# A gate unit between the value units, two levels of masks drawn ahead, and decay rows in two parts, in the gated delta stage of a two-block decoder

## The reference

```python
def c_mixer(h, w_in, conv_w, a_log, dt_bias, head_gain, w_out):
    qkv, gate, b, a = _split(h @ w_in, C_SIZES)
    qkv = jax.nn.silu(short_conv(qkv, conv_w))
    ...
    o = gated_deltanet(q, k, v, beta, log_alpha)
    o = rmsnorm(o, head_gain) * jax.nn.silu(gate.reshape(B, T, GDN_HEADS, GDN_DV).astype(jnp.float32))
    return o.reshape(B, T, GDN_VW) @ w_out

def gated_deltanet(q, k, v, beta, log_alpha):
    g = jnp.cumsum(_to_chunks(log_alpha.astype(f32), L), axis=-1)
    decay = jnp.where(incl, jnp.exp(g[..., :, None] - g[..., None, :]), 0.0)
    kk = jnp.einsum('nbhtd,nbhsd->nbhts', kc, kc)
    lower = jnp.where(strict, bc[..., :, None] * kk * decay, 0.0)
    rhs = jnp.concatenate([vc * bc[..., None], kc * (bc * jnp.exp(g))[..., None]], axis=-1)
    sol = lax.linalg.triangular_solve(lower + eye, rhs, ...)
    attn = jnp.einsum('nbhtd,nbhsd->nbhts', qc, kc) * decay
    ...  # then a scan over the chunks
```

## Time and profile before

| | |
|---|---|
| median of 3 runs | 1335.72 us (1333.64 to 1336.63) |
| profiled execution, its own time | 1339.24 us |
| its span, first to last instruction | 1337.2 us |
| PE busy | 1279.0 us (96%) |
| weight loads on PE | 1161.5 us (87%) |
| DVE, ACT, POOL busy | 790.7, 707.8, 128.2 us (59%, 53%, 10%) |
| mean granted TensorE clock | 0.984 |
| read from HBM | 203.05 MB, 153 GB/s over the span |

### The profile page before, as it was taken

One profiled execution on the slowest core, in us unless ns is written; L12 is line 12 of the kernel. 1 busy time (PEld: TensorE's weight loads), 2 busy tenths in 40 slices (PEclk: granted clock), 3 DMA queues, 4 the chain that ended last, 5 costly groups with the idle time before them and its releaser, 6 DMA issues.

```text
span 1337.2 us, 22102 instructions
## 1 busy us (share of the span) xinstructions
PE 1279.0 (96%) x9192; PEld 1161.5 (87%) x9192; DVE 790.7 (59%) x1159; ACT 707.8 (53%) x1115; POOL 128.2 (10%) x146
## 2 busy tenths in 40 slices
PE   6999999999999979999999999998999999999997
PEld 6988899998889868888998888988997888999886
DVE  5776678885456565655554447784555645555444
ACT  5766666664476434645555336562355544655443
POOL 5000001110000000000111000106500000111000
PEclk9999999999999999999999999997999999999999
DMA  9433455555544523533655554541112543455550
GB/s 331 154 113 117 142 190 186 177 176 203 188 126 174 189 95 126 189 127 98 198 179 189 193 182 147 173 140 48 66 33 83 186 158 126 158 181 178 194 200 37
DMA packets 141430, 205.53 MB, mean 154 GB/s; under 512 B 3730, under 2 KB 118802, under 8 KB 141330
## 3 DMA queue, kind: packets, MB, share of 16 engines
q1 hardware_dynamic: 141330, 204.11, 46.0%
HBM read 203.05 MB, written 1.05 MB: 153 GB/s over the span
## 4 chain that ended last, share of the span: by engine, by line
PE 85%; DVE 7%; ACT 4%; issue 2%; DMA 1%; SPq 0%; POOL 0%; ACTq 0%; DVEq 0%
PE ps L301 41%; PE ps L363 26%; PE ps L381 5%; PE ps L2055 2%; DVE weights_lo L280 2%; PE ps L1703 1%; PE ps L2120 1%; ACT weights_hi L277 1%; PE ps L1725 1%; PE ps L2006 1%; PE ps L2010 1%; PE ps L485 1%; DVE split_arena L516 1%; ACT normed L902 1%; DMA weights<-in_w_in 1%
## 5 line engine op out<-in xcount | busy, mean ns | idle before, releaser
L280 DVE TENSOR_TENSOR weights_lo<-weights,weights_hi 128x1024 fp32r<-128x1024 f32 x379 | 471.3, 1255 | 248.9 <-ACT weights_hi L277 247.0
L301 PE MATMUL ps<-split_arena,weights_hi 128*128 128x256 f32 x3056 | 565.8, 287 | 7.9 <-DVE split_arena L516 7.0
L277 ACT ACTIVATE weights_hi<-weights 128x1024 fp32r<-128x1024 f32 x379 | 396.7, 1057 | 267.1 <-PE ps L363 183.0
L301 PEld LDWEIGHTS ps<-split_arena,weights_hi 128*128 128x128 f32 x3056 | 483.2, 194 | 16.2 <-issue 11.9
L301 PE MATMUL ps<-split_arena,weights_lo 128*128 128x256 f32 x1528 | 435.5, 285 | 0.0
L301 PEld LDWEIGHTS ps<-split_arena,weights_lo 128*128 128x128 f32 x1528 | 296.5, 194 | 0.0
L363 PE MATMUL ps<-weights_hi,split_arena 128*128 128x512 f32 x992 | 272.6, 392 | 5.1 <-DVE arena L1649 3.0
L363 PEld LDWEIGHTS ps<-weights_hi,split_arena 128*128 128x128 f32 x992 | 184.5, 188 | 44.4 <-issue 6.1
L363 PE MATMUL ps<-weights_lo,split_arena 128*128 128x512 f32 x496 | 153.6, 390 | 0.0
L363 PEld LDWEIGHTS ps<-weights_lo,split_arena 128*128 128x128 f32 x496 | 93.1, 188 | 19.6
L1883 POOL TENSOR_TENSOR normed<-normed 128x512 f32<-128x512 f32 x32 | 34.1, 1065 | 502.9 <-ACTq L1875 502.9
(11 more groups left out here) (358 smaller groups left out, 1332.8 us busy)
## 6 DMA issues: line engine op xcount, KB each, us to landing
weights<-in_mlp_w SPq DMA_DIRECT2D x64, 1024.0 KB, 5.4
weights<-in_w_up SPq DMA_DIRECT2D x22, 1024.0 KB, 5.1
weights<-in_c_w_in SPq DMA_DIRECT2D x16, 1024.0 KB, 5.5
weights<-in_w_in SPq DMA_DIRECT2D x14, 1024.0 KB, 6.2
weights<-in_ab_w_in SPq DMA_DIRECT2D x12, 1024.0 KB, 5.3
weights<-in_w_down SPq DMA_DIRECT2D x11, 1024.0 KB, 5.0
weights<-in_xa_wv SPq DMA_DIRECT2D x8, 1024.0 KB, 4.9
weights<-in_xa_wq SPq DMA_DIRECT2D x8, 1024.0 KB, 5.3
```

The source lines that it names most:

```text
L277: act.activation(h, r, ACT.Copy).then_inc(s_hi, 1)
L280: dve.tensor_tensor(l, r, h.bitcast(F32), ALU.subtract).then_inc(s_lo, 1)
L301: mm = pe.matmul(o, w[:, k, :], x[:, k, :], start=(k == 0 and i == 0), stop=(k == DC - 1 and i == 2))
```

## The change

The stage computes the same with its work placed otherwise:

- **Order of units.** The first gate unit comes between the value units, as `c_gate0`, and its columns go to bank 4; ACT copies them out before `products(0)`. The gate columns are turned between the two parts of the last value unit, and DVE copies them out ahead of its last `conv`. What was `gate_part(0)` and `(1)` is gone; `gate_part(2)` to `(7)` keep their numbers. The key tile of one part (`keys(1, 1)`) comes ahead of that of two.
- **Decay rows.** `CRK` and `CRQ` are split by DVE into high and low fp32r parts (`RBK`, `RBQ`); `products(n)` takes two heads at all 256 tokens instead of four heads at 128, as four fp32r matmuls of 128x256, whose stationary operand is a column of an 8x8 identity, repeated (`SELR`).
- **Masks.** POOL makes levels 0 and 1 of `hg` 0, then both of `hg` 1, then the two subtractions (`XT`). `products(4)` moves ahead of level 1.
- **Splits.** In levels 1 to 4 the parts that are split are one further along the list than before (`GP0 + 7 + lvl`), so ACT's high part there waits for the `gate_part` of its own level; the split before the scan is gone.
- **End.** Head squares and sums have four buffers, three head sums come first, then the key tile of one part, the fourth head sum and the key tile of two parts; DVE and ACT copy them out in that order.

```diff
-            cols("c_qkv", "c_w_in", [*range(1024, 2048, 256), *range(0, 1024, 256), *range(2048, 3072, 256)])
-            cols("c_gate", "c_w_in", range(3072, 4096, 256))
-            keys(1, 0, 1)
+            cols("c_qkv", "c_w_in", [*range(1024, 2048, 256), *range(0, 1024, 256), 2048, 2304])
+            cols("c_gate0", "c_w_in", [3072])
+            cols("c_v", "c_w_in", [2560, 2816])
+            cols("c_gate", "c_w_in", range(3328, 4096, 256))
+            keys(1, 1, 0)
...
-        CRK, CRQ = PIN_t[0:8, 0, :], PIN_t[0:8, 1, :]
+        CRK, CRQ = GS[1], GS[2]
+        RBK = view(44 * 256, (2, T), 8, of=split_arena)
+        RBQ = view(46 * 256, (2, T), 8, of=split_arena)
+        SELR = sb("head_rows", [8, 8], F32R)
...
-        GP0 = first_part[first_unit["c_gate"]]
+        GP0 = first_part[first_unit["c_gate"]] - 2
...
+        def unit_at(u):
+            return ("c_qkv", u) if u < 10 else ("c_v", u - 10)
+
+        def heads_at(n):
+            return n % 4 // 2, n % 2 * 2
...
-            for u in range(NCU):
-                cols_unit("c_qkv", u, HT, G + u % 4, free)
+            def gate_columns():
+                pe.wait_ge(named("c_row"), 2)
+                for t in range(TT):
+                    pe.transpose(PS[:, A + 3, 72 * t:72 * t + 72], GAB[:, t * P:(t + 1) * P], ident[0:72, 0:72])
+                pe.matmul(PS[:, A + 3, 144:152], ones[0:8, :], DG[:, :], start=True,
+                          stop=True).then_inc(named("c_cols"), 1)
+
+            for u in range(NCU - 1):
+                if u == 10:
+                    cols_unit("c_gate0", 0, HT, A)
+                stage, i = unit_at(u)
+                cols_unit(stage, i, HT, G + u % 4, lambda _i: free(u))
                 for i in SQUARES_AFTER.get(u, ()):
                     sum_squares(i)
...
+            free(11)
+            cols_part(first_unit["c_v"] + 1, 0, HT, G + 3)
+            gate_columns()
+            cols_part(first_unit["c_v"] + 1, 1, HT, G + 3)
 
             def products(n):
...
-                hg, c = n // 2 % 2, n % 2
-                r, q0 = (CRK, 8) if n < 4 else (CRQ, 0)
+                hg, j0 = heads_at(n)
+                r, q0 = (RBK, 8) if n < 4 else (RBQ, 0)
                 if n == 0:
                     pe.wait_ge(named("c_silu"), 8)
+                    pe.wait_ge(named("c_ge"), 1)
...
-                for j in range(4):
-                    mm = pe.matmul(PS[:, MB[n], j * P:(j + 1) * P], sel[:, 4 * hg + j, :], r[:, tok(c)], start=True,
-                                   stop=True)
+                for i in range(2):
+                    h = 4 * hg + j0 + i
+                    one = SELR[:, h:h + 1].to_broadcast([8, P])
+                    for x in range(2):
+                        mm = pe.matmul(PS[:, MB[n], i * T:(i + 1) * T], one, r[:, x, :], start=(x == 0),
+                                       stop=(x == 1))
                 mm.then_inc(named("c_p"), 1)
...
             products(0)
             products(1)
             products(2)
-            gate_part(0)
+            gate_part(2)
             products(3)
-            gate_part(1)
-            gate_part(2)
-
-            pe.wait_ge(named("c_lt"), 2)
+            gate_part(3)
+
+            pe.wait_ge(named("c_lt"), 3)
             pe.wait_ge(named("c_prep"), 2)
             blocks(6, lambda r, hg, m: LT[r, 0, hg, m, :], lambda r, hg, m: ident[r, r], "c_ym")
-            gate_part(3)
+            products(4)
 
             for lvl in range(1, LEVELS):
                 pe.wait_ge(named("c_x"), 2 * lvl)
                 pe.wait_ge(named("c_lt"), 2 * lvl + 2)
-                if lvl == 1:
-                    pe.wait_ge(named("c_prep"), 3)
                 blocks(2, lambda r, hg, m: LT[r, lvl % 2, hg, m, :], lambda r, hg, m: XI[r, hg, m, :], "c_ym")
                 if lvl < 5:
-                    products(3 + lvl)
+                    if lvl > 1:
+                        products(3 + lvl)
                     gate_part(3 + lvl)
                     value_turn(lvl - 1)
                     pe.wait_ge(named("c_prep"), 4 + lvl)
...
-                    if lvl % 2 == 0:
-                        pe.wait_ge(named("c_tq"), lvl // 2)
+                    pe.wait_ge(named("c_tq"), lvl)
...
 
             head_sums(0)
             head_sums(1)
-            key_pe(1, 0, 4)
             head_sums(2)
+            key_pe(1, 1, 5)
             head_sums(3)
-            key_pe(1, 1, 5)
+            key_pe(1, 0, 4, lambda: pe.wait_ge(named("c_rs"), 3))
...
+            act.wait_ge(s_const, 2)
+            act_then(act.activation(SELR[:, :], ident[0:8, 0:8], ACT.Copy))
             for u in range(NCU):
-                cols_done(act, "c_qkv", u)
+                if u == 10:
+                    cols_done(act, "c_gate0", 0)
+                    act.activation(SGT[:, 0:2, :], PS[:, A, :].rearrange("p (c n) -> p c n", c=2),
+                                   ACT.Copy).then_inc(named("c_ge"), 1)
+                cols_done(act, *unit_at(u))
...
-            split(act, GP0 + 3)
+            split(act, GP0 + 5)
             decays(3)
             act.wait_ge(named("c_row"), 3)
...
-            split(act, GP0 + 4)
-            gate_evac(0)
-            split(act, GP0 + 5)
             split(act, GP0 + 6)
             gate_evac(1)
+            decays(4)
+            query_decay(0)
+            split(act, GP0 + 7)
             for lvl in range(1, LEVELS):
                 y_high(lvl)
                 if lvl < 5:
-                    decays(3 + lvl)
-                    if lvl % 2 == 0:
-                        query_decay(lvl // 2 - 1)
-                    split(act, GP0 + 6 + lvl)
+                    if lvl > 1:
+                        decays(3 + lvl)
+                        query_decay(lvl - 1)
+                    split(act, GP0 + 7 + lvl)
...
+            for b in range(4):
+                head_squares(b)
+            for b in range(3):
+                head_roots(b)
             out_high(0)
-            key_evac(1, 0, act, 4)
-            head_roots(2)
             out_high(1)
             head_roots(3)
-            split(act, GP0 + 13)
+            split(act, GP0 + 12)
             out_high(2)
             out_high(3)
+            split(act, GP0 + 13)
+            key_evac(1, 0, act, 4)
...
-            for lvl in range(LEVELS):
+            def masked(lvl, hg):
+                for b in range(2):
+                    r = slice(64 * b, 64 * b + 64)
+                    ins = pool.tensor_tensor(LT[r, lvl % 2, hg, :, :], ATC[r, hg, :, r],
+                                             LM[r, lvl, r].unsqueeze(1).to_broadcast([64, 8, 64]), ALU.mult)
+                ins.then_inc(named("c_lt"), 1)
+
+            pool.wait_ge(named("c_silu"), NCU)
+            for hg in range(2):
+                pool.wait_ge(named("c_prep"), 2 * hg + 2)
+                masked(0, hg)
+                masked(1, hg)
+            for hg in range(2):
+                pool.wait_ge(named("c_lt"), 4)
+                pool_then(pool.tensor_tensor(XT[:, hg, :, :], idb, LT[:, 0, hg, :, :], ALU.subtract))
+                pool.sem_inc(named("c_xt0"), 1)
+            for lvl in range(2, LEVELS):
...
+                dve_then(dve.tensor_copy(RBK[:, 0, :], CRK))
+                dve.tensor_tensor(RBK[:, 1, :], CRK, RBK[:, 0, :].bitcast(F32), ALU.subtract)
...
+                dve_then(dve.tensor_copy(RBQ[:, 0, :], CRQ))
+                dve_then(dve.tensor_tensor(RBQ[:, 1, :], CRQ, RBQ[:, 0, :].bitcast(F32), ALU.subtract))
...
-            for u in range(NCU):
+            for u in range(NCU - 1):
                 conv(u)
                 if u == ROWS_AFTER:
                     gate_rows()
-
             dve.wait_ge(named("c_cols"), 1)
             dve_then(dve.tensor_copy(GCB[:, :, :], PS[:, A + 3, 0:144].rearrange("p (t n) -> p t n", t=2)))
             dve_then(dve.tensor_tensor(GX[:, 0, :], PS[:, A + 3, 144:152], GCB[:, 0, 0:8], ALU.subtract))
             dve.sem_inc(named("c_row"), 1)
+            conv(NCU - 1)
...
             exponents(1)
             decayed(0)
             exponents(2)
-            split(dve, GP0 + 3)
             decayed(1)
             exponents(3)
             decayed(2)
             decayed(3)
-            split(dve, GP0 + 4)
             split(dve, GP0 + 5)
+            split(dve, GP0 + 6)
...
-            split(dve, GP0 + 6)
+            exponents(4)
+            decayed(4)
+            split(dve, GP0 + 7)
...
-                if lvl < 5:
+                if 1 < lvl < 5:
                     exponents(3 + lvl)
                     decayed(3 + lvl)
-                    split(dve, GP0 + 6 + lvl)
+                if lvl < 5:
+                    split(dve, GP0 + 7 + lvl)
...
-            split(dve, GP0 + 12)
             out_low(0)
             gate_out(2)
             out_low(1)
-            split(dve, GP0 + 13)
+            key_evac(1, 1, dve, 5)
+            split(dve, GP0 + 12)
             gate_out(3)
             out_low(2)
-            key_evac(1, 1, dve, 5)
```

(1 more changed line is left out.)

106 lines of the change are left out of this document (39 added, 67 removed).

## The result

| | before | changed |
|---|---|---|
| median, runs on one chip | 1336.57 us (7 runs, 1333.64 to 1341.07) | 1329.45 us (7 runs, 1326.29 to 1330.54) |
| ratio of times, 95% interval | | 0.994 (0.9924 to 0.9956) |
| profiled execution, its own time | 1339.24 us | 1329.45 us |
| its span | 1337.2 us | 1327.6 us |
| mean granted clock | 0.984 | 0.985 |

The change makes the kernel faster, by 0.6% or some 8 us (5.9 to 10.2 by the interval; the two medians differ by 7.1). The forecast was 1324.3 with 1319.5 to 1331.0: the time is inside, 5.2 us above the forecast.

A forecast was written before the change was run, and what follows sets the result against it. PE, busy for 96% of the span, was the bound, with 16.4 us of idle time and half clock between 883.17 and 941.79. Gains of 7.8 + 0.9 + 2.7 = 11.4 us off the median 1335.72 gave 1324.3, range 1319.5 to 1331.

The forecast's parts named there:

- A: From the start of the eleventh unit to level 1's blocks(4): 7.8 us gained, bounds 3.4 to 10.2.
- A, columns: PE idles 0.8 us ahead of the first value unit's second part, 0.4 ahead of products(2), where 2.9 stood.
- A, spreading rows: In products, four fp32r matmuls take 0.5 us instead of 1.06; 0.121 us each, upper bound 0.28.
- A, masks: Level 0's blocks(6) waits for six half masks: 6.3 us idle, start 920.8; two splits meeting masks add 1.8.
- A, clock: Clock falls in PE's idle before blocks(6), returns 8 to 9 us after PE resumes; level 1's blocks(4) at 934.0.
- B: Levels 2 to 4: products 0.56 us shorter each, less 0.8 us lost; gain 0.9 us, bounds -0.5 and 1.7.
- The feared delay of X: Levels 1 and 2: DVE's low-part split meeting a mask delays X by 0.7 us, 0.3 hidden; 0.8 us lost.
- C: End of the stage: of c_out's 2.8 us wait for a key tile copy 0.1 stays; gain 2.7, bounds 1.2 and 2.8.
- the first two rivals: Clock low through level 1: 1328.7, chance 0.15; all masks slow, X late in all levels: 1329.1, chance 0.08.

The follow-up runs named there:

- fp32 rows: Changed kernel with decay rows spread by fp32 matmuls of 256 columns, without DVE's four extra gate-row instructions; 1326.94 us, ratio to before 0.9927.
- changed kernel's second trace: Profile of the changed kernel timed again with no edit; median 1328.73 us, ratio to before 0.9939, stage 145.2 us.
- end alone: Kernel before with only four buffers of head squares and sums and the new end order of key tiles, copies and units; 1333.04 us, ratio 0.9977.
- the second execution: Profile of the kernel before, run again with no edit; median 1338.37 us, ratio 1.0013, stage 154.0 us.
- the old masks: Changed kernel with POOL's mask order of before (level 0 of both groups, subtractions, then level 1); 1329.23 us, ratio to before 0.9932.

## Why the prediction was right, and where its sizes were off

The direction, the mechanism and each place that it named hold. The sizes are off in places, and some of the agreement is luck.

- **A, columns.** 0.8 us of idle ahead of the value part: 0.71. 0.4 ahead of `products(2)`: 0.21, a little less because the rows took longer.
- **A, spreading rows.** I priced them at 0.121 us each by L301. They take 0.67 / 4 = 0.17 us: type and width were not all that sets them. It lies between my bounds, but the upper one, 0.28, was an fp32 matmul of 128 columns; of 256 columns it takes 0.53 (two in 1.06 us, in "fp32 rows"). It cost 0.2 us per `products`, hidden in the first four.
- **A, masks.** `blocks(6)` at 920.8 forecast, 921.09 measured; its wait 6.3 forecast, 5.8 measured. The charge of 1.8 us for two splits is 1.7 by experiment, and masks beside other work of DVE were not slow: in the changed kernel's second trace four that ran beside the copy of Y, exponents and `decayed` of level 2 took 5.31 us, 1.33 each. By the rule in the Trainium skill, "GPSIMD Engine Reference", section 1, splits with two SBUF inputs contend and exponents out of PSUM do not; these rows agree.
- **A, clock.** Back 8 to 9 us after PE resumed, I said; it was 929.8 - 921.1 = 8.7. I had taken that from one low stretch of the trace of before, and other waits brought 3.4 or 13.6 us, so part of this agreement is luck. `blocks(4)` at 934.0 forecast, 934.23 measured. My bounds doubled the work for half clock; the rows show less, 3.68 for 2.08 us of `blocks` and 0.64 for 0.36 of three matmuls of a weight part. A is 58.6 - 51.1 = 7.5 us against 7.8.
- **B.** 0.9 forecast. From `blocks(4)` of level 1 to the start of the scan, the two traces differ by 0.5 us: the dearer rows took 3 x 0.17 back. The feared delay of X showed once, as 0.45 us in level 2.
- **C.** 2.7 forecast; from the start of the scan to L383 it was 1037.23 - 985.88 = 51.35 and is 1026.49 - 977.83 = 48.66, 2.7 us less, and 3.1 by the ratio of "end alone".

The sum by traces is 10.7 of 11.4 us. The step that failed is the last, "the median before is 3.5 lower, 1335.72, and 1324.3 is the forecast". The profiled execution of before had 23.8 us at half clock in the stage; another execution of it had 17.0, and a stage 1.9 us shorter, while the changed kernel's stage repeated within 0.1. So the sum was worked out against an execution that had lost more to the clock than the other one did, and taking the whole of it off the lower median counted that loss twice. Against the second execution A is 55.2 - 51.1 = 4.1 us, and the rest of the stage gains 4.7 instead of 3.2, since there half clock stood behind the wait of `c_out`. The stage then gains 8.8 us (154.0 - 145.2), close to the 8.1 by ratio.

The 5.2 us between forecast and median are then made up so: 0.7 by the terms of the sum (11.4 against 10.7), 1.9 by the execution that was profiled (10.7 against 8.8), 1.7 between 8.8 and the 7.1 of the medians, and 0.9 because the median before rose to 1336.57 with four more runs. The last two are within the scatter and have no cause shown; that the typical run has a stage like the second execution's rests on that one trace. With both traces at hand, a forecast near 1328 would have been right for the median.

The two ends of the range were also not added up as stated: the lower bounds of the three terms give 3.4 - 0.5 + 1.2 = 4.1 us, not 4.5. And the median of 1329.45 lies nearer to the first two rivals (1328.7 and 1329.1) than to the forecast. Neither happened: the clock was back before `blocks(4)` of level 1, and only masks beside a split were slow. That their numbers fit is chance.

The runs also showed where gain was left: 5.8 us of idle and 10.2 us at half clock behind it, worth 5 to 6 us with two gate parts moved. The forecast had named that wait and taken it as given.

Open: what sets the length of a low stretch, 3.4, 10.2 or 13.6 us behind waits of like size, and whether there is one. Whether "fp32 rows" gets the short one always, or did so in its profile only, can't be told from one trace; its median suggests that it often does. And by no run was the new place of the gate unit and the value units tried alone; that the wait of 2.9 us went by it is read from the traces. The experiments bound it from the other side: the stage of the changed kernel is 4.6 us shorter than with the end alone, and neither the old masks (3.2 left) nor the fp32 rows take that back.

## What to carry to other kernels

Every wait of over 4 us on TensorE had half clock behind it here, a second price of 1.3 to 3.9 us where it was worked out: give such a wait work before shortening what it waits for. Faster work ahead of a wait that another engine ends only makes the wait longer, and what it costs the other engine can make it longer still: the new rows lengthened it by 0.3 us in the one way and 1.0 in the other. Where a profiled execution is slower than its median, look for half clock in it before taking differences off the median.

## What the runs showed of the hardware that was not expected

- The length of a half-clock stretch behind a wait of PE, worked out from stretches of 4 us: about 10.2 us behind 5.8 (two traces), 6.2, 4.1, 4.6 (one trace) and 2.9 us of idle (two traces); 3.4 behind 4.5, 4.6 (two traces), 2.8 (one trace) and 2.5 (two traces); 13.6 behind the wait of 2.9 in the first trace of before. Waits of 2.98, 2.39 and 2.19 us brought none, nor did that of 2.8 in the first trace of before.
- An fp32r matmul 8 partitions deep and 256 columns wide, with a repeated column as stationary operand, takes 0.17 us at full clock, where the 128 deep ones of L303 take 0.12; the fp32 matmul of the same width takes 0.53 (two, which are four records, in 1.06).
- A DVE split and POOL's half masks slow each other: a split takes 2.24 us instead of 1.18, and each split adds 0.87 us to the masks.
